# RWKV-7 recurrence of a hybrid decoder step: triangular products by output half, diagonal blocks copied by ScalarE, the state's update at the end of TensorE's step

## What is computed

```python
def wkv7_scan(r, w, k, v, a, b, s0):
    def step(S, inp):
        rt, wt, kt, vt, at, bt = inp
        S = (S * wt[:, :, None, :] + jnp.einsum('bhvk,bhk->bhv', S, at)[..., None] * bt[:, :, None, :]
             + vt[..., None] * kt[:, :, None, :])
        return S, jnp.einsum('bhvk,bhk->bhv', S, rt)
    ...
```

## Time and profile before

| | us |
|---|---|
| median of 3 runs | 3277.62 (3275.03 to 3281.9) |
| the profiled execution | 3286.38 |
| its span | 3284.2 |
| PE busy | 3041.3 (93%) |
| DVE, ACT, POOL busy | 1586.4, 930.9, 1384.1 |
| recurrence, first VectorE instruction to last product of item 15 | 1844.1 to 2396.6 |

### The profile page before, as it was taken

The page is one execution under the profiler, slowest core; times in us unless marked ns, Lnnn a source line. Parts: engine busy times, 40 slices in busy tenths (PEclk is TensorE's granted clock), DMA queues, the critical chain, the costliest instruction groups (busy, mean ns, idle before and its releaser), DMA issues.

```text
span 3284.2 us, 74630 instructions
## 1 busy us (share of the span) xinstructions
PE 3041.3 (93%) x32844; PEld 2848.5 (87%) x32844; DVE 1586.4 (48%) x2107; ACT 930.9 (28%) x1560; POOL 1384.1 (42%) x1047
## 2 busy tenths in 40 slices
PE   7999988989999999979999788888878999999997
PEld 6989856979999999969999776776668999999996
DVE  5032264138666631254122355777623776664125
ACT  4132265232111111134111255555433311111111
POOL 2323320226777743512433333444433477774320
PEclk8999998899999999989999889999989999999998
DMA  3353443221233343213322222212052222323311
GB/s 99 122 133 111 153 160 114 80 96 59 80 83 116 84 140 120 53 64 142 124 90 92 76 63 76 71 53 70 21 187 77 78 78 78 110 78 136 136 42 62
DMA packets 342475, 312.31 MB, mean 95 GB/s; under 512 B 35335, under 2 KB 303059, under 8 KB 341020
## 3 DMA queue, kind: packets, MB, share of 16 engines
q1 hardware_dynamic: 325706, 275.99, 27.7%
q10 hardware_dynamic: 16466, 31.83, 2.6%
HBM read 212.79 MB, written 94.62 MB: 94 GB/s over the span
## 4 chain that ended last, share of the span: by engine, by line
PE 40%; DVE 6%; issue 4%; ACT 1%; SPq 1%; DMA 1%; POOL 1%; ACTq 0%; DVEq 0%; POOLq 0%
PE PS L521 17%; PE PS L688 12%; PE PS L2814 2%; PE PS L2820 1%; PE PS L2826 1%; PE PS L2804 1%; PE PS L2808 1%; PE PS L702 1%; DVE act_lo L2516 1%; PE PS L2800 1%; SPq L496 0%; PE PS L2961 0%; DMA rw<-z_st 0%; PE PS L708 0%; DVE g_AK L3272 0%
## 5 line engine op out<-in xcount | busy, mean ns | idle before, releaser
L521 PE MATMUL PS<-act_hi,w_hi 128*128 128x344 f32 x1992 | 641.1, 322 | 38.0 <-DVE act_lo L2150 22.0
L521 PE MATMUL PS<-act_lo,w_hi 128*128 128x344 f32 x1992 | 637.7, 320 | 0.0
L521 PE MATMUL PS<-act_hi,w_lo 128*128 128x344 f32 x1992 | 637.2, 320 | 0.0
L502 POOL CAST w_hi<-w_raw 128x1024 fp32r<-128x1024 f32 (+1 forms) x119 | 127.3, 1070 | 1086.3 <-PE PS L521 559.2
L521 PEld LDWEIGHTS PS<-act_hi,w_hi 128*128 128x128 f32 x1992 | 376.3, 189 | 43.6 <-issue 29.3
L521 PEld LDWEIGHTS PS<-act_hi,w_lo 128*128 128x128 f32 x1992 | 376.3, 189 | 0.0
L521 PEld LDWEIGHTS PS<-act_lo,w_hi 128*128 128x128 f32 x1992 | 376.3, 189 | 0.0
L688 PE MATMUL PS<-T,wq_S 128*128 128x258 f32 x2880 | 365.7, 283 | 0.0
L688 PE MATMUL PS<-act_hi,wq_A 128*128 128x258 f32 x1920 | 364.5, 282 | 0.0
L688 PEld LDWEIGHTS PS<-T,wq_S 128*128 128x128 f32 x2880 | 354.4, 189 | 0.0
L688 PEld LDWEIGHTS PS<-act_hi,wq_A 128*128 128x128 f32 x1920 | 305.4, 190 | 0.0
(11 more groups left out here) (609 smaller groups left out, 6014.6 us busy)
## 6 DMA issues: line engine op xcount, KB each, us to landing
hidd<-hid_out SPq DMA_DIRECT2D x44, 516.0 KB, 3.3
w_raw<-in_ffn_w_gate_dram SPq DMA_DIRECT2D x44, 512.0 KB, 4.8
w_raw<-in_ffn_w_up_dram SPq DMA_DIRECT2D x44, 512.0 KB, 6.1
w_raw<-in_ffn_w_down_dram SPq DMA_DIRECT2D x32, 512.0 KB, 3.7
...
```

The lines of the kernel that those rows point to most:

```text
L502: nc.gpsimd.tensor_copy(w_hi[:, u, 0:kts, :], w_raw[:, u, 0:kts, :]).then_inc(w_hi_done, 1)
L521: mm = nc.tensor.matmul(PS[:, 3 * u + c, 0:CH], w[:, u, kt, :], x[:, kt, CH * c:CH * c + CH], start=(kt == 0 and part == 0), stop=(kt == k ...
```

## The change

- **Products by output half.** AK V is two matmuls per head, one from the upper 64 rows to the upper output half (L2872 of the kernel after), one from all 128 rows to the lower output half (L2873). Both heads of a pair go to their own bank, 6 + e. A S is one matmul per head on 64 rows and 128 columns. u is likewise two matmuls per head, `i_X11` (64 rows) and `i_XC` (128 rows: X21 above X22), into bank 6. The two matmuls with zeros, the two ScalarE copies (`rhs7`, `u7`) and the two VectorE adds go; VectorE copies both right sides straight from PSUM.
- **Diagonal blocks.** ScalarE copies the 32x32 diagonal blocks into `i_X11`, `i_XC` (4 copies, "xd") and `i_Xa` (2 copies, "xa"). GpSimd's two masked products go; three buffers are zeroed by it once, ahead of the loop.
- **Order.** pX32 moves to the front of the next step, pBU (the state's update) behind pY to the end, pN before pX16, RKV before pT16, ptK before pRB, pkk before pRK. On ScalarE t64 and y come ahead of the stage's exponentials and of t. On VectorE the state's sum and product come later, A and B of an item end the step before the one in which they began it. On GpSimd kp and rk are made in stage s after R, and o follows sum at once.

Core of the diff (the lists of the other engines are reordered in the same way):

```diff
-        BG = Order(sem("sc_pool"), "rkm:i b:s sum:o diag:i xad:i kp:p R:s rk:p o:o", AHEAD, -3, ITEMS + 1, ITEMS)
+        BG = Order(sem("sc_pool"), "R:s kp:s rk:s rkm:i b:s sum:o o:o", AHEAD, -3, ITEMS + 1, ITEMS)
-        BA = Order(sem("sc_act"), "nc:i t32:n n:i w21:n tB:i x21:n t:s t64:n sq:s t2:i iP:s pe0:s tK:i rhs7:n rkc:i t4:i y:o ln:s ysq:o rs:s u7:n t8:i yln:o D:n yrs:o t16:i tV:s ygn:o", AHEAD, -3, ITEMS + 1, ITEMS)
+        BA = Order(sem("sc_act"), "tV:i sq:s t16:n nc:i n:i t32:n xd:n xa:n w21:n tB:i x21:n t64:n y:o pe0:s iP:s t:s t2:i tK:i rkc:i t4:i ysq:o ln:s rs:s t8:i yln:o yrs:o D:n ygn:o", AHEAD, -3, ITEMS + 1, ITEMS)
-        BV = Order(sem("sc_dve"), "A:i B:i xs16:n x16:n cs:s mid:s st:o dm:n S:o ct:i cc:s ak:i xi:i xt:i bv:i tr:n rb:i xs2:i x2:i rhs:n ss:s xs4:i K:s x4:i kkn:s u:n xs8:i x8:i yn:o", AHEAD, -3, ITEMS + 1, ITEMS)
+        BV = Order(sem("sc_dve"), "x16:n ct:i cs:s xi:i mid:s dm:n st:o S:o cc:s bv:i xt:i ak:i tr:n rb:i xs2:i x2:i K:s ss:s rhs:n xs4:i x4:i u:n kkn:s yn:o xs8:i x8:i B:s A:s xs16:i", AHEAD, -3, ITEMS + 1, ITEMS)
-        BP = Order(sem("sc_pe"), "pAK:i pT64:n pbon:i pX64:n pAS:n pT2:i pRB:i ptK:i pX2:i pRK:i pT4:i pkk:s pX4:i pcen:o pU:n pT8:i pvar:o pX8:i ptV:s pT16:i pX16:i pN:s pBU:n ptB:s pT32:i pX32:i pY:n", AHEAD, -3, ITEMS + 1, ITEMS)
+        BP = Order(sem("sc_pe"), "pX32:n pAK:i pT64:n pbon:i pX64:n pAS:n pT2:i ptK:i pRB:i pX2:i pkk:s pRK:i pT4:i pcen:o pX4:i pU:n pT8:i pvar:o pX8:i ptV:s pT16:i pN:s pX16:i ptB:s pT32:i pY:n pBU:n", AHEAD, -3, ITEMS + 1, ITEMS)
...
-                    mm(PS[half(0), 7, 0:GP * DH], nothing, S[half(1), :, :].rearrange("p q v -> p (q v)"), start=True, stop=False, skip_group_check=True)
-                    for h in range(GH):
-                        V = [t_V[half(a), n % 3, P * (h % GP) + DH * (h // GP):P * (h % GP) + DH * (h // GP) + DH] for a in range(2)]
-                        for a, b in ((0, 0), (1, 1), (0, 1)):
-                            mm(part(h, a, b), g_AK[half(a), n % 2, h, half(b)], V[a], start=(h == 0), stop=False, skip_group_check=True)
-                        ins = mm(PS[half(0), 3, DH * h:DH * h + DH], i_T64[half(1), h, :], i_XD[half(1), h, :], start=True, stop=True)
+                    for q in range(GP):
+                        for e in range(2):
+                            h, col, v = GP * e + q, slice(DH * q, DH * q + DH), slice(P * q + DH * e, P * q + DH * e + DH)
+                            mm(PS[half(0), 6 + e, col], g_AK[half(0), n % 2, h, half(0)], t_V[half(0), n % 3, v], start=(q == 0), stop=False, skip_group_check=True)
+                            mm(PS[half(1), 6 + e, col], g_AK[:, n % 2, h, half(1)], t_V[:, n % 3, v], start=(q == 0), stop=False, skip_group_check=True)
+                            ins = mm(PS[half(0), 3, DH * h:DH * h + DH], i_T64[half(1), h, :], i_XC[half(1), h, :], start=True, stop=True)
...
-                        for e, b in ((0, 0), (1, 1), (0, 1), (1, 0)):
-                            ins = mm(part(GP * e + q, e, b), f_A[half(e), n % 2, q, half(b)], S[half(e), q, :], start=False, stop=True, skip_group_check=True)
+                        for e in range(2):
+                            ins = mm(PS[:, 6 + e, DH * q:DH * q + DH], f_A[half(e), n % 2, q, :], state(n)[half(e), q, :], start=False, stop=True, skip_group_check=True)
...
-                    mm(PS[half(0), 7, :], nothing, flat(q_rhs)[half(1), :], start=True, stop=True, skip_group_check=True)
-                    for h in range(GH):
-                        rhs = [q_rhs[half(a), h // GP, h % GP, :] for a in range(2)]
-                        mm(part(h, 0, 0), i_XD[half(0), h, :], rhs[0], start=(h == 0), stop=True, skip_group_check=True)
-                        mm(part(h, 1, 1), i_XD[half(1), h, :], rhs[1], start=(h == 0), stop=True, skip_group_check=True)
-                        ins = mm(part(h, 0, 1), i_X21[half(0), h, :], rhs[0], start=(h == 0), stop=True, skip_group_check=True)
+                    for e in range(2):
+                        for q in range(GP):
+                            h = GP * e + q
+                            mm(PS[half(0), 6, DH * h:DH * h + DH], i_X11[half(0), h, :], q_rhs[half(0), e, q, :], start=True, stop=True)
+                            ins = mm(PS[half(1), 6, DH * h:DH * h + DH], i_XC[:, h, :], q_rhs[:, e, q, :], start=True, stop=True)
```

More of the change, by code:

```diff
@@ L2556, in decoder_step @@
         i_X, i_T = room("i_X", [P, 2, 2, GH, 32]), room("i_T", [P, GH, 32])
-        i_XD, i_X21, i_Xa, i_T64 = (room(f"i_{n}", [P, GH, DH]) for n in ("XD", "X21", "Xa", "T64"))
+        i_X11, i_XC, i_Xa, i_T64 = (room(f"i_{n}", [P, GH, DH]) for n in ("X11", "XC", "Xa", "T64"))
         q_rhs, q_u = room("q_rhs", [P, 2, GP, DH]), room("q_u", [P, 2, GP, DH])
@@ L2827, in level_X @@
                 return ins
-            part = lambda h, a, b: PS[half(b), 6 + a, DH * h:DH * h + DH]
             state = lambda j: q_S[:, j % NG, (j // NG) % 2, :, :]
-            nothing = m_incl[half(1), 0:DH]
             pe.wait_ge(VM.sem, len(VM.names) + START)
@@ L2838, in scan_tensor @@
                 live_p, live_s, live_i, live_n, live_o = (0 <= j < ITEMS for j in (p, s, i, n, o))
+                if live_n:
+                    pe.wait_ge(BA.sem, BA.of("t32", n))
+                    X = i_X[:, n % 2, 1, :, :]
+                    for h in range(GH):
+                        mm(PS[quad(0), 3, 32 * (GH + h):32 * (GH + h) + 32], i_T[quad(1), h, :], X[quad(1), h, :], start=True, stop=True)
+                        mm(PS[quad(2), 3, 32 * (GH + h):32 * (GH + h) + 32], i_T[quad(3), h, :], X[quad(3), h, :], start=True, stop=True)
+                        ins = mm(PS[quad(1), 3, 32 * h:32 * h + 32], X[quad(1), h, :], i_T[quad(1), h, :], start=True, stop=True)
+                    ins.then_inc(BP.sem, BP.turn("pX32", n))
                 if live_i:
@@ L2951, in scan_tensor @@
                     turn(f_in["v"][:, s % 2, :, :]).then_inc(BP.sem, BP.turn("ptV", s))
-                if live_i:
-                    pe.wait_ge(BV.sem, BV.of("x8", i))
-                    level_T(4, i).then_inc(BP.sem, BP.turn("pT16", i))
                 if live_n:
@@ L2963, in scan_tensor @@
                 if live_i:
-                    pe.wait_ge(BA.sem, BA.of("t16", i))
-                    level_X(i).then_inc(BP.sem, BP.turn("pX16", i))
+                    pe.wait_ge(BV.sem, BV.of("x8", i))
+                    level_T(4, i).then_inc(BP.sem, BP.turn("pT16", i))
                 if live_s:
@@ L2971, in scan_tensor @@
                     scores(0, f_B, f_A[:, s % 2, :, :]).then_inc(BP.sem, BP.turn("pN", s))
-                if live_n:
-                    pe.wait_ge(BV.sem, BV.of("u", n))
-                    pe.wait_ge(BA.sem, BA.of("tB", n))
-                    for q in range(GP):
-                        for e in range(2):
-                            col = slice(P * q + DH * e, P * q + DH * e + DH)
-                            ins = mm(PS[half(e), 7, DH * q:DH * q + DH], t_B[:, n % 2, col], q_u[:, e, q, :], start=False, stop=True, skip_group_check=True)
-                    ins.then_inc(BP.sem, BP.turn("pBU", n))
+                if live_i:
+                    pe.wait_ge(BA.sem, BA.of("t16", i))
+                    level_X(i).then_inc(BP.sem, BP.turn("pX16", i))
                 if live_s:
@@ L2983, in scan_tensor @@
                     turn(f_B).then_inc(BP.sem, BP.turn("ptB", s))
+                if live_n:
+                    for q in range(GP):
+                        for e in range(2):
+                            mm(PS[half(e), 5, P * q:P * q + P], state(n)[half(e), q, :], f_R[half(e), n % 3, q, :], start=False, stop=False, skip_group_check=True)
                 if live_i:
@@ L3009, in scan_tensor @@
                     ins.then_inc(BP.sem, BP.turn("pY", n))
+                    pe.wait_ge(BV.sem, BV.of("u", n))
+                    pe.wait_ge(BA.sem, BA.of("tB", n))
+                    for q in range(GP):
+                        for e in range(2):
+                            col = slice(P * q + DH * e, P * q + DH * e + DH)
+                            ins = mm(PS[half(e), 7, DH * q:DH * q + DH], t_B[:, n % 2, col], q_u[:, e, q, :], start=False, stop=True, skip_group_check=True)
+                    ins.then_inc(BP.sem, BP.turn("pBU", n))
             pe.wait_ge(BV.sem, BV.of("S", ITEMS - 1))
@@ L3257, in scan_vector @@
                 if live_o:
+                    new, old = q_S[:, o % NG, (o // NG + 1) % 2, :, :], q_S[:, o % NG, (o // NG) % 2, :, :]
+                    dve.wait_ge(BP.sem, BP.of("pBU", o))
+                    tt(new, PS[:, 7, 0:DH * GP].rearrange("p (q v) -> p q v", v=DH), old, ALU.add).then_inc(BV.sem, BV.turn("st", o))
                     new = q_S[:, o % NG, (o // NG + 1) % 2, :, :]
@@ L3314, in scan_vector @@
                     turn_X(2, i)
[L3315 to L3324 removed]
+                piece(3)
                 if live_s:
```

302 lines of the change are left out of this document (135 added, 167 removed).

## The result

The changed kernel takes 3327.88 us (median of 4 runs, 3324.3 to 3334.04), the kernel before 3276.32 us beside it: ratio 1.0157 (95% interval 1.0135 to 1.0179), 51.6 us slower. The prediction was 3337 us with 3300 to 3372.

What follows compares the result with a forecast made beforehand. TensorE was taken to bound each 32.35 us step. Shapes +5.4 less 1.4 gave +4.0 us, times 15 is 60; less 2.7 at the end, plus 2 at the start, +59: 3337 us, range 3300 to 3372.

Steps and rivals of the forecast that it cites:

- The price of a change of shape: TensorE matmuls alternating 64*64 and 128*64: 0.26 us for a run of one matmul, bounds 0.20 and 0.30.
- The product for u: TensorE group of L2916 and L2917: 16 runs, 4.15 us where it took 1.6, +2.5 us per step.
- The first group: AK V and products with the state: 4.15 plus 0.85, together 5.0 us against 1.94, +3.05 us per step.
- the sum: Extra TensorE time per step from changes of shape: +5.4 us, bounds +3.5 and +7.
- Idle from issue: TensorE short of instructions, mostly among quick matmuls: 0.7 of 3.5 us per step goes, bounds 0 and 1.5.
- most idle is inside the levels, which stay: Argument against the rival that slower groups win back all 4.5 us idle per step (3292 us, chance 0.08).
- Waits: TensorE's waits, mainly 0.5 us per step ahead of L2876, go with the new order: 0.7 us off.
- the loop on VectorE that I feared: Rival: a late wait on VectorE or ScalarE adds 1 to 2 us per step, 3352 to 3367; chance 0.05.
- the rival: TensorE's granted clock is low 20% of the time, not 8%: some 2 us more per step, 3367 us; chance 0.12.
- Per step: Recurrence step: +5.4 for shapes less 1.4 for waits and idle, +4.0 us, to 36.4; forecast range +2.0 to +5.5.
- The start: Ahead of the recurrence, three more memsets and R stand before kp on GpSimd: +2 us, from +1.5 to +3.
- The end: GpSimd finishes item 13's output sooner, -2.7 us; SP's weight loads, 15.86 us, cover step 15.

Runs made afterwards that it cites:

- e2: The changed kernel with its matmuls sorted by shape in both product groups, in place of alternating shapes: 3241.34 us, ratio 0.9901 to the kernel before.
- e3: The kernel before with the change's products by output half, sorted by shape, in the old order: 3272.65 us, ratio 0.9993 to the kernel before.
- e7: The changed kernel sorted by shape, with 32 more matmuls once ahead of the steady steps (half an instruction block): 3257.86 us, ratio 0.9939.
- e1: The kernel before with only the products by output half, shapes by turns, in the old order: 3367.37 us, ratio 1.0276 to the kernel before.
- e4: The kernel before with the product pcen done five times in place of once, as filler: 3313.77 us, ratio 1.0122 to the kernel before.
- e6: The changed kernel sorted by shape, with 16 more matmuls once ahead of the steady steps (a quarter of an instruction block): 3254.21 us, ratio 0.9923.
- e10: The changed kernel sorted by shape, with the 24 quick matmuls of pX32 issued twice in a row: 3264.7 us, ratio 0.9968 to the kernel before.
- e12: The changed kernel with the old products by quarters, zeros, ScalarE's bank 7 copies and VectorE's adds, keeping order and diagonal blocks: 3249.19 us, ratio 0.9916.

## Where the prediction was right and where wrong

- **The price of a change of shape: right.** 0.26 us for a run of one matmul, measured 0.257. The product for u was to hold TensorE 4.15 us and holds it 4.11. The first group was to take 5.0 and takes 5.44: it has 17 runs where I counted 16 (2139.76 - 2135.35 = 4.41), and the products with the state turned to 64*128 take 1.03, near the upper bound of 1.09 and not the 0.85 that I took. The two groups alone are 3.5 + 2.5 = 6.0 us longer than before, and the work rose by an estimated 5.3; the sum had 5.4. The rule cited from the Trainium skill, TensorEngine Tiling (Array Packing), Key Properties, is that mode switching requires a drain. The traces agree for the pair 64*64 and 128*64, which no row of before had shown: 0.14 us per change (e2).
- **Idle from issue: mis-sized.** "Of 3.5 us I take off 0.7, bounds 0 and 1.5": it lost 3.0. I had the right place, the quick matmuls, but thought of slower groups that give time back, and so of a small part of the idle time. The runs show that most of it goes with the form of the products, also where they are sorted (e3: 3.5 to 1.2). That "most idle is inside the levels, which stay" was the step that failed: it sits in the levels and hangs on the groups beside them. As for the Trainium skill, Runtime: NRT & Kernel Launch, Instruction fetch mechanics, "mostly hidden" fits the changed kernel (0.5 us in 7 crossings per step) and not before (3.5) or a border inside pX16 (e7, 1.26 to 1.49 us each).
- **Waits: the right one, half the size.** 0.7 us off was taken; the wait of 1.48 us ahead of the group is gone, and the waits are 0.35 us less. Idle time was to be near 3 us per step and is 1.2. The state's sum and product are hidden, no wait on L3236 or its product shows ahead of L2872. Of the loop on VectorE that I feared, 0.2 us per step remains ahead of L2916.
- **The clock: it did fall, by less than the rival had.** 0.96 to 0.94 over the steps, 0.8 us per step more lost, where the rival asked for 2. In e1 it does what the rival says and more, 0.87. In the changed kernel the first group runs at full clock in every step but the last; the order, or the diagonal blocks that go with it, made that difference.
- **Per step:** +5.3 of work, +0.8 of clock, -3.3 of idle make +2.8, the prediction +5.4 - 1.4 = +4.0. The 60 us of 15 steps are 20 too much against the 39.5 measured. That 3337 lies only 9 us over 3327.88 is luck in part: an error at the end of 9 us the other way made up for half of it, and the rest is of the size by which executions of one kernel differ.
- **The start: wrong in sign.** +2 us was expected; pY of item 0 comes 8.3 us earlier. Windows from 1840 to pY of item 0, before, after, and below them e4, whose list up to there is that of before but for the filler:

```profile
1840.00:1924.20 84.20, 63.41 (x1654) 55.01 (x1652) 45.87 (x75) 35.72 (x74) 29.55 (x21) 0.72 0.21 48
...
1840.00:1915.90 75.90, 54.60 (x1512) 45.68 (x1512) 40.35 (x73) 36.77 (x78) 24.94 (x21) 0.82 0.28 67
```

```profile
1840.00:1915.48 75.48, 54.62 (x1629) 47.00 (x1629) 44.15 (x73) 34.67 (x73) 28.03 (x21) 0.77 0.23 54
```

  e4 has it at 1915.5, 8.7 us ahead of before. Over all profiles this start lies between 1910.5 and 1929.5, and mostly later where more was lost to the clock up to there (77 us in before, 58 in after, 61 in e4). So I take it for a difference between executions and not for an effect of the change; it would also be most of the 10 us by which the profiled execution of before lay over its median.
- **The end: wrong in sign.** -2.7 was expected, and step 15 "is covered by" the weight loads. From pY of item 14 to the first L521 it is 46.1 us in place of 39.5, +6.6. SP's list after:

```profile
2410.77 15.62 SPq L496 DMA_DIRECT2D w_raw<-in_rwkv_w_o_dram  x2
2440.57 3.66 SPq L2677 DMA_DIRECT2D mix<-e_yt  x8
```

  The weights are issued by 2426.4, and then SP waits 14 us for the samples' rows, which stand behind VectorE's yn of item 14 and so behind TensorE's step 15. That step has both groups by turns at half clock, in the chain that ended last:

```profile
2424.72 0.40 PE PS L2916 x2
...
2425.53 0.40 PE PS L2916 x2
```

  two matmuls in 0.81 us where 0.51 stood in the steps. The cover of 16 us that the sum leaned on was real for a step 15 of 17.6 us and not for one of 31.0. Where step 15 is short in the new order (15.9 to 19.8 us in e2, e6, e7, e10 and e12), the same stretch is 36.1 to 37.4 us, 2 to 3 less than before: there the -2.7 comes true.

- **Slips in the working.** Between two starts of L2881 lie three other passes and not six; a head has eight, so the 0.115 us per head stands. Of the chain in the earlier trace rows the recurrence's lines are 7 points and L521 and L688, which are not the recurrence, 29; that TensorE bounds a step rests on the earlier trace rows. With all its own bounds (3.5 to 7, less 0.7, less 0 to 1.5) a step comes to +1.3 to +6.3 us and the time to 3296 to 3371, wider than the 3306 to 3360 written down.

By parts, from the medians: order and ScalarE's diagonal blocks together -27 us (e12; of its 2.1 us per step the table puts 1.3 to the clock, 0.6 to waits and 0.6 to issue, against 0.4 more work); the products by output half -8 when sorted (e2 against e12; within what the place of the borders does); by turns +87 (after against e2). Together +52. The last term is the turns' own time (3.8 us per step) and the clock (1.8) less 0.3 of idle, 74 us in 14 steps, with 9 more at the end (46.1 against 37.4). The order and the diagonal blocks were not taken apart. The time of the prediction is closer than its terms: it won too little idle, and had an end gain that lost.
